# Forget gates of a streaming encoder step: the bias column among the constants, a reciprocal next to a logarithm, and decay rows spread from SBUF

## What is computed

```python
proj = h @ w_in
q, k, v, fl = jnp.split(proj, [D_C, 2 * D_C, 3 * D_C], axis=-1)
logf = jax.nn.log_sigmoid(fl + b_f)                 # (tokens, 16)
# prompt: dq = dk = cumsum(logf);   sample: keys are 256 cached rows, then the 32 new ones
dpast = jnp.cumsum(clf, axis=1); dpast = dpast - dpast[:, -1:]
s = einsum('bqhd,bkhd->bhqk', q, k) * ATTN_SCALE
s = s + dq[..., :, None] - dk[..., None, :]         # then causal mask, softmax, times v
```

## Time and profile before

| | us |
|---|---|
| median of 3 runs | 2401.23 |
| lowest and highest | 2400.63, 2403.25 |
| the profiled execution | 2400.34 |
| its span | 2398.5 |
| PE busy | 2318.9 (97% of the span) |
| DVE busy | 1455.9 (61%) |
| ACT busy | 908.8 (38%) |
| POOL busy | 306.0 (13%) |

### The profile page before, as it was taken

The page is one execution under the profiler, slowest core; times in us unless marked ns, Lnnn a source line. Parts: engine busy times, 40 slices in busy tenths (PEclk is TensorE's granted clock), DMA queues, the critical chain, the costliest instruction groups (busy, mean ns, idle before and its releaser), DMA issues.

```text
span 2398.5 us, 45405 instructions
## 1 busy us (share of the span) xinstructions
PE 2318.9 (97%) x18804; PEld 2219.7 (93%) x18804; DVE 1455.9 (61%) x2667; ACT 908.8 (38%) x1968; POOL 306.0 (13%) x369
## 2 busy tenths in 40 slices
PE   7999999999998999999999999998999999999998
PEld 4999999978887999999999999997888789999998
DVE  5477758666667756656566665656666675533223
ACT  4322233355566422222442222333655563222232
POOL 0000002321114300001220000123011161000001
PEclk8999999999999999999999999998999999999999
DMA  8356545422223144545514454541333222433331
GB/s 256 113 167 174 170 127 168 119 69 81 80 74 92 45 133 141 150 120 164 149 44 137 136 159 125 164 127 53 90 103 109 82 80 74 138 97 89 90 92 51
DMA packets 392700, 277.66 MB, mean 116 GB/s; under 512 B 11104, under 2 KB 349824, under 8 KB 392496
## 3 DMA queue, kind: packets, MB, share of 16 engines
q1 hardware_dynamic: 385792, 254.77, 36.4%
q0 software_dynamic: 6704, 19.99, 2.9%
HBM read 263.48 MB, written 12.81 MB: 115 GB/s over the span
## 4 chain that ended last, share of the span: by engine, by line
PE 87%; DVE 7%; ACT 2%; issue 2%; DMA 2%; POOL 0%; SPq 0%; ACTq 0%; DVEq 0%; POOLq 0%
PE lin L1035 64%; PE lin L1292 10%; PE lin L1055 2%; PE ps_s L1344 2%; PE ps_o L1425 2%; PE ps_t L1366 1%; DVE acc L2023 1%; PE ps_t L1315 1%; DMA raw<-in_ffn_w_down 1%; DVE x L2108 1%; PE ps_s L1111 1%; DVE h_lo L2135 1%; DVE neg_max L2458 1%; DVE sums L2070 1%; ACT w_hi L1539 1%
## 5 line engine op out<-in xcount | busy, mean ns | idle before, releaser
L1035 PE MATMUL lin<-h_hi,w_hi 128*128 128x272 f32 x2640 | 568.0, 290 | 3.0 <-ACT work L1619 2.1
L1035 PE MATMUL lin<-h_hi,w_lo 128*128 128x272 f32 x2640 | 565.1, 289 | 0.0
L1035 PE MATMUL lin<-h_lo,w_hi 128*128 128x272 f32 x2640 | 563.0, 288 | 0.0
L1984 DVE TENSOR_TENSOR w_lo<-raw,w_hi 128x1024 fp32r<-128x1024 f32 (+1 forms) x263 | 319.9, 1221 | 311.0 <-ACT w_hi L1539 309.5
L1035 PEld LDWEIGHTS lin<-h_hi,w_hi 128*128 128x128 f32 x2640 | 422.8, 189 | 5.1 <-ACT work L1619 2.8
L1035 PEld LDWEIGHTS lin<-h_lo,w_hi 128*128 128x128 f32 x2640 | 423.4, 189 | 0.0
L1035 PEld LDWEIGHTS lin<-h_hi,w_lo 128*128 128x128 f32 x2640 | 420.6, 189 | 0.0
L1539 ACT ACTIVATE w_hi<-raw 128x1024 fp32r<-128x1024 f32 (+1 forms) x263 | 270.0, 1036 | 181.2 <-DMA raw<-in_ffn_w_down 143.3
L2023 DVE SCALAR_TENSOR_TENSOR acc<-raw,silu_c,acc 128x512 f32<-128x512 f32 x448 | 313.7, 759 | 0.0
L1035 PE MATMUL lin<-act_hi,w_hi 128*128 128x272 f32 x1296 | 284.9, 290 | 5.9 <-DVE w_lo L1984 5.9
L1035 PE MATMUL lin<-act_hi,w_lo 128*128 128x272 f32 x1296 | 283.2, 290 | 0.0
(11 more groups left out here) (327 smaller groups left out, 3454.3 us busy)
## 6 DMA issues: line engine op xcount, KB each, us to landing
raw<-in_w_ada SPq DMA_DIRECT2D x128, 512.0 KB, 3.8
raw<-in_ffn_w_gate SPq DMA_DIRECT2D x88, 512.0 KB, 3.8
raw<-in_ffn_w_up SPq DMA_DIRECT2D x88, 512.0 KB, 3.8
raw<-in_ffn_w_down SPq DMA_DIRECT2D x64, 448.0 KB, 4.2
raw<-in_ffn_w_down SPq DMA_DIRECT2D x32, 512.0 KB, 4.8
raw<-in_w_in_ab SPq DMA_DIRECT2D x24, 512.0 KB, 3.9
raw<-in_w_in_c SPq DMA_DIRECT2D x24, 512.0 KB, 3.8
start_w<-in_w_ada SPq DMA_DIRECT2D x16, 512.0 KB, 12.0
```

The lines of the kernel that those rows point to most:

```text
L1035: m = nc.tensor.matmul(out[a], w_tile(w, k), mv[:, k0 + k, half(a)], start=first and k == 0 and n == 0, stop=last and k == u["tiles"] - 1 ...
L1984: nc.vector.tensor_tensor(w_all(w_l, u["tiles"]), raw_all(u, w_l), w_all(w_h, u["tiles"]).bitcast(F32), ALU.subtract).then_inc(lo_done, 1)
```

## The change

It has three parts. The bias column gets a place outside the region that the sub-layers share (in the place of `b_warm`, whose one use moves to a free column of `warm`), and is loaded with the constants at the start; DVE waits for it on a semaphore of its own. In `forget_gate` the reciprocal writes `e_t` and is issued without waiting for ACT's logarithm, the correction is applied to min(z, 0) first and the logarithm subtracted last, and the `ones16` fill stands ahead of the wait for ACT's exponential. The DRAM copy of `decay` is gone: each of the 16 transfers into `dk_b` reads one row of `decay` in SBUF, that is one partition, 128 times.

```diff
-        b_warm = sb("b_warm", [P, 1])
+        bf_col = sb("bf_col", [16, 1])
...
             pool.dma_start(rel_in[:], relpos[0]).then_inc(rel_dram, 16)
+            pool.dma_start(bf_col[:], b_f.rearrange("a h -> h a")).then_inc(bf_in, 16)
...
                         if st.st == 0:
                             pool.wait_ge(fl_done, FL_DECAY)
-                            pool.dma_start(dec_scratch[:, :], decay[:]).then_inc(fl_dram, 16)
-                            pool.wait_ge(fl_dram, 16)
                         for hh in range(2):
+                            hd = 2 * st.tile_of(0) + hh
                             pool.dma_start(dk_b[:, st.new, hh, :],
-                                           dec_rows[2 * st.tile_of(0) + hh].broadcast_to([P, SEQ + PAST + DEC])
+                                           decay[hd:hd + 1, :].rearrange("p (o n) -> p o n", o=1).broadcast_to([1, P, SEQ + PAST + DEC])
                                            ).then_inc(dk_in[st.new], 16)
...
                     pool.dma_start(clf_nat[:], cc_logf[0, 0].rearrange("(t q) h -> q t h", q=P)).then_inc(fl_in, 16)
-                    pool.dma_start(bf_col[:], b_f.rearrange("a h -> h a")).then_inc(fl_in, 16)
...
                 def logits(a):
-                    dve.wait_ge(fl_in, 32)
+                    dve.wait_ge(bf_in, 16)
...
                 fl(nc.vector.scalar_tensor_tensor(e_t[:], z_t[:], -1.0, z_t[:], ALU.mult, ALU.min))
+                fl(nc.vector.memset(ones16[:], 1.0), False)
                 dve.wait_ge(fl_act, 1)
                 fl(nc.vector.tensor_scalar(u_t[:], e_t[:], 1.0, None, ALU.add))
 
                 fl(nc.vector.scalar_tensor_tensor(logf[:], u_t[:], -1.0, e_t[:], ALU.add, ALU.subtract))
+                fl(nc.vector.reciprocal(e_t[:], u_t[:]))
+                fl(nc.vector.tensor_tensor(e_t[:], e_t[:], logf[:], ALU.mult))
+                fl(nc.vector.scalar_tensor_tensor(z_t[:], z_t[:], 0.0, e_t[:], ALU.min, ALU.add))
                 dve.wait_ge(fl_act, 2)
-                fl(nc.vector.reciprocal(u_t[:], u_t[:]))
-                fl(nc.vector.tensor_tensor(logf[:], logf[:], u_t[:], ALU.mult))
-                fl(nc.vector.tensor_tensor(l_t[:], l_t[:], logf[:], ALU.subtract))
-                fl(nc.vector.scalar_tensor_tensor(logf[:], z_t[:], 0.0, l_t[:], ALU.min, ALU.subtract))
-                fl(nc.vector.memset(ones16[:], 1.0))
+                fl(nc.vector.tensor_tensor(logf[:], z_t[:], l_t[:], ALU.subtract))
```

More of the change, by code:

```diff
@@ L243, in program @@
     rel_scratch = nc.dram_tensor("rel_scratch", (8, P, 384), F32, kind="Internal").ap()
-    dec_scratch = nc.dram_tensor("decay_scratch", (16, SEQ + PAST + DEC), F32, kind="Internal").ap()
     def job_d(n, u):
@@ L414, in program @@
         clf_nat = sb("clf_nat", [P, 2, 16])
-        bf_col = sb("bf_col", [16, 1])
         logf = sb("logf", [16, TOK])
@@ L559, in program @@
         fl_in = sem("fl_in")
+        bf_in = sem("bf_in")
         fl_ps = sem("fl_ps")
-        fl_dram = sem("fl_dram")
         dk_in = [sem(f"dk_in{k}") for k in range(2)]
@@ L976, in kv @@
                         pool.dma_start(ds[st.tile_of(0)], src[0:DEC, st.new, QT, :]).then_inc(kv_stored[st.new], 16)
-            dec_rows = dec_scratch.rearrange("h (o n) -> h o n", o=1)
             pool.wait_ge(rel_done, 2)
@@ L1443, in stage @@
                         pe.wait_ge(var_done, 2 * st.j + 2)
-                        pe.wait_ge(fl_in, 32)
+                        pe.wait_ge(fl_in, 16)
                         for t in range(2):
@@ L1825, in forget_act @@
                 nc.scalar.activation(e_t[:], e_t[:], ACT.Exp).then_inc(fl_act, 1)
-                act.wait_ge(fl_done, 4)
+                act.wait_ge(fl_done, 5)
                 nc.scalar.activation(l_t[:], u_t[:], ACT.Ln).then_inc(fl_act, 1)
@@ L1908, in stage @@
                     if att == "b" and st.st == 8 and s == 13:
-                        nc.scalar.activation(b_warm[:, 0:1], eps[:, 0:1], ACT.Sqrt)
+                        nc.scalar.activation(warm[:, 2:3], eps[:, 0:1], ACT.Sqrt)
                     if st.new is not None:
```

## The result

| | before | after |
|---|---|---|
| median of 6 runs each, us | 2400.97 | 2472.26 |
| lowest and highest | 2400.10, 2403.25 | 2459.00, 2477.24 |
| the profiled execution | 2400.34 | 2459.00 |
| its span | 2398.5 | 2457.2 |

The ratio is 1.0287, with a 95% interval from 1.0259 to 1.0316: slower by 71 us, where 40 were forecast, and 7 us above the range. The profiled execution is the quickest of the six; what is read from it explains 59 us.

The account below looks back on a forecast made before the run. The prediction took PE as the bound (87% of the span in the chain that ended last). It summed 23.9 + 2 + 14 = 40 us, gate gain included, onto 2400.34: 2440, as a median 2441, range 2395.5 to 2465.

Parts of the forecast that it names:

- The gate: Early bias column, reciprocal not waiting for the logarithm, and moved fill: decay done 0.55 + 0.79 + 0.71 = 2.05 us earlier.
- The rate of a row: Reads from one SBUF partition run at 24.7 GB/s: 33.2 us a pair plus 1.7 landing, 34.9; this case's chance 0.55.
- one sixteenth of the path: All 128 reads share one partition, limited to what one of 16 DMA engines carries at full load, 24.7 GB/s.
- as fast as from DRAM: Rival: SBUF rows land in 6.73 us or the median 4.7, giving 2397.4 down to 2395.7 us; chance 0.39.
- one at a time: Rival: rows leave their partition singly, 90 us a pair, over 400 us more; priced from 2500 up, chance 0.06.
- The first stall: PE at stage 1's first transposes: 23.9 us later for the first pair, plus 2 us for the low clock afterwards.
- the second pair: Queued behind the first, it lands at 1734.6, when stage 2 wants it, and costs nothing.
- The later stages: From stage 3 on, waits for rows of 4.5, 0.8, 3.7, 0.8, 3.7, 0.8 us, together 14 us.
- The weights are drawn in: Slow rows delay weight loads: up to 2 us a stage, 14 in all, 2455; upper part of the 0.55 case's range.

Follow-up runs that it names:

- e1: Changed kernel with all decay rows from a DRAM copy again, early bias column and reordered gate kept: 2398.59 us, 0.9993 of before.
- e9: Changed kernel, only the first pair from SBUF, each transfer reading partitions 0 and 1, 64 times each; later pairs from DRAM: 2425.85 us, 1.0105 of before.
- e10: Changed kernel, only the first pair from SBUF, each transfer reading partitions 0 and 8; later pairs from DRAM: 2410.43 us, 1.0034 of before.
- e3: Changed kernel with only the first pair of rows from SBUF, the seven later pairs from a DRAM copy: 2423.01 us, 1.0096 of before.
- e4: Changed kernel with the first pair of rows from a DRAM copy, the seven later pairs from SBUF: 2457.78 us, 1.0245 of before.
- e8: Changed kernel with only the second head's row of each later pair from SBUF, all other rows from DRAM: 2398.74 us, 0.9996 of before.

## Why the prediction was wrong

**The gate: right.** 2.05 us forecast, 1.98 in the trace. That it doesn't show by the median (e1: 1.8 us, interval across 1) follows from its size.

**The rate of a row: right, and its time in part by luck.** 24.7 GB/s was taken from one sixteenth of the path; the trace has 28, and issue to DVE's start is 34.2 us for 34.9. At 28 GB/s the pair is served in 29.3 us, so the rows are quicker than was taken, and 4.9 us go to issue, landing and other transfers, where 1.7 were taken; the two errors cancel. The estimate that the prediction worked out from the Trainium skill, 29.7 us, has the rate closer, and with 1.7 us of landing the time less so. That the sixteenth is what binds, and not the partition, the prediction took without a row that shows it; e9 and e10 bear it out. Of the rivals, "as fast as from DRAM" and "one at a time" fall with it.

**The first stall: right.** 23.9 and 2 us were forecast over the kernel before, with the gate's gain counted in; e3 lies 22.7 us above it (and 24.4 above e1). From `h_hi` to DVE's first add it is 57.3 us in the kernel after and 34.1 before, 23.2 more. The time needed by the second pair was hidden as forecast: stage 2 is 31.93 us long.

**The later stages: this step failed.** The sum took 14 us, from waits for `dk_b` in six stages. (With each pair queued behind the one before, the same terms give 15, and by the rate of the Trainium skill the whole sum is some 15 us smaller, not 12; neither changes the case.) In the profiled execution the kernel was 23.7 us late when stage 2 began (1730.68 for 1707.01 on POOL) and 58.9 at the end of stage 8 (1988.60 for 1929.68). Of these 35 us DVE's later waits for `dk_b` are only 7.4, and PE stood 5.0 behind them: while PE stood for other reasons, the rows caught up. The rest is what the prediction had as *The weights are drawn in* and priced at up to 2 us a stage, because three loads were thought ready in 36 us. Two things were missing in that price. A weight tile that comes late stops PE (8.1 us once) and what is then behind it, and each pause is paid again in clock: 10.4 us of PE's work in four stages. And a queue was overlooked: the instructions, 150 packets that no table of loads lists. Late fetches made 11.5 us here, and 52 in e4's profiled execution. With two slow rows per stage the DMA engines have next to no free time left, so every small transfer waits; e8, with one, shows no loss, so the price is not proportional.

The direction and its cause (third part, single partition) were as forecast; the size was 71 us and not 40. Why the time scatters by 18 us from run to run, 28 in e4, is not settled; late fetches that sometimes find a gap would do it, but it was not tried.

## What to carry to other kernels

A row that is spread to 128 partitions should not be read 128 times from one partition of SBUF: the copy to DRAM costs 2.3 us once, the direct reads 15 us per 400 KB. Before a transfer is called hidden, add up the time that it holds the DMA engines, not its bytes: near a share of 1 (here 0.87 to 1.01) it was the weights and the instruction fetches that stopped the kernel, and at 0.66 to 0.75 nothing did. A pause without a releaser can be tested for a late fetch by counting: it then stands a whole number of instruction packets behind the last one. And a test of two sources needs both in one transfer, or a look at the landings, since two queues need not run side by side.

## What the runs showed that had not been expected

- Reads of one partition, or of it and its neighbour, came at 28 to 30 GB/s, whether they held the engines all the time or a quarter of it; a second partition eight further made it 53.
- PE paused 1.5 to 17 us with no semaphore behind it. Each pause of that kind ended 2.2 to 2.7 us after a 16 KB packet of the instruction queue began, and in three kernels they stand at the same places of PE's program, multiples of 256 instructions apart.
- A row issued on ACT's queue was served to its end before POOL's, issued 0.8 us later, had its turn: 17.2 and 30.8 us to landing.
